# Expert gate and up matrices of two experts in one 4 MB load, and a TensorE loop over the two pairs of a turn

## The reference

```python
def run_block(args):
    xb, e = args
    h = jax.nn.silu(xb @ w_gate[e]) * (xb @ w_up[e])   # w_gate[e], w_up[e]: 1024 x 512
    return h @ w_down[e]                               # w_down[e]: 512 x 1024
y = jnp.zeros((N, D), x.dtype).at[slot_tok].add(ys * slot_gate[:, None])
```

## Time and profile before

| what | value |
|---|---|
| median of 3 runs | 1482.35 us (1481.81 to 1485.76) |
| the profiled execution | 1482.48 us |
| its span, first to last instruction | 1480.7 us |
| TensorE busy | 1235.6 us, 83% |
| VectorE, ScalarE busy | 496.0 us, 293.6 us |
| bytes read by DMA | 491.39 MB |
| mean granted TensorE clock | 0.946 of full |

### The profile page before, as it was taken

One profiled execution on the slowest core, in us unless ns is written; L12 is line 12 of the kernel. 1 busy time (PEld: TensorE's weight loads), 2 busy tenths in 40 slices (PEclk: granted clock), 3 DMA queues, 4 the chain that ended last, 5 costly groups with the idle time before them and its releaser, 6 DMA issues.

```text
span 1480.7 us, 34399 instructions
## 1 busy us (share of the span) xinstructions
PE 1235.6 (83%) x15164; PEld 947.1 (64%) x15164; DVE 496.0 (33%) x1038; ACT 293.6 (20%) x740; POOL 53.2 (4%) x89
## 2 busy tenths in 40 slices
PE   9999977677767777686777786877799999999998
PEld 6566756556556556565555565655678687888854
DVE  1663222122121120221221202212278555566644
ACT  3433221012021120210111202101232222211100
POOL 4101000000000000000000000000010110000000
PEclk9999999899899997998999989989999999999999
DMA  9539999999999999999999999999993351555420
GB/s 343 193 140 380 381 428 428 428 428 428 428 429 428 429 428 429 428 429 428 429 428 428 428 428 429 428 428 428 408 336 114 128 184 59 171 171 170 171 85 29
DMA packets 79759, 493.01 MB, mean 333 GB/s; under 512 B 4924, under 2 KB 28696, under 8 KB 55144
## 3 DMA queue, kind: packets, MB, share of 16 engines
q1 hardware_dynamic: 77792, 486.69, 80.1%
q0 software_dynamic: 1520, 4.91, 1.1%
q10 hardware_dynamic: 408, 0.86, 0.2%
HBM read 491.39 MB, written 1.05 MB: 333 GB/s over the span
## 4 chain that ended last, share of the span: by engine, by line
DMA 53%; PE 44%; DVE 1%; issue 1%; ACT 0%; POOL 0%; SPq 0%; DVEq 0%; POOLq 0%
DMA ring<-in_w_gate_dram 46%; PE bank L1678 8%; PE bank L1230 6%; DMA ring<-in_w_down_dram 5%; PE bank L881 4%; PE bank L1725 4%; PE bank L1358 4%; PE bank L1043 2%; DMA ring<-in_w_up_dram 2%; PE bank L1544 1%; PE bank L805 1%; PE bank L1654 1%; PE bank L1407 1%; PE bank L781 1%; PE bank L1587 1%; PE bank L1624 1%
## 5 line engine op out<-in xcount | busy, mean ns | idle before, releaser
L1230 PE MATMUL bank<-ring,big 128*32 128x128 f32 x8192 | 302.6, 309 | 176.0 <-DMA ring<-in_w_gate_dram 117.6
L1230 PEld LDWEIGHTS bank<-ring,big 128*32 128x32 f32 x8192 | 261.3, 125 | 226.8 <-DMA ring<-in_w_gate_dram 89.0
L2592 DVE TENSOR_TENSOR big<-big,bank 128x128 f32<-128x128 f32 x64 | 24.1, 376 | 498.5 <-PE bank L1230 498.5
L1259 PE MATMUL bank<-ring,big 128*32 128x256 f32 x1536 | 101.0, 406 | 33.6 <-DMA ring<-in_w_down_dram 33.1
L1982 ACT ACTIVATE big<-bank 32x256 f32<-32x256 f32 x96 | 35.9, 374 | 388.9 <-PE bank L1259 387.7
L2604 DVE COPY big<-bank 32x256 f32<-32x256 f32 x96 | 40.5, 422 | 195.7 <-PE bank L1259 194.2
L1259 PEld LDWEIGHTS bank<-ring,big 128*32 128x32 f32 x1536 | 50.3, 114 | 65.0 <-issue 28.3
L1245 PEld LDWEIGHTS bank<-aux,c 128*128 128x128 f32 x512 | 65.5, 200 | 15.0 <-issue 15.0
L1245 PE MATMUL bank<-aux,c 128*128 x512 | 74.3, 290 | 0.0
L881 PE MATMUL bank<-ring,xT 128*128 128x512 f32 (+1 forms) x160 | 67.9, 563 | 0.2 <-DVE xT L2231 0.2
L1205 PE MATMUL bank<-big,xn 128*128 128x128 f32 x512 | 65.1, 288 | 0.0
(11 more groups left out here) (482 smaller groups left out, 1691.3 us busy)
## 6 DMA issues: line engine op xcount, KB each, us to landing
ring<-in_w_up_dram SPq DMA_DIRECT2D x64, 2048.0 KB, 26.8
ring<-in_w_gate_dram SPq DMA_DIRECT2D x63, 2048.0 KB, 26.0
ring<-in_w_down_dram SPq DMA_DIRECT2D x62, 2048.0 KB, 27.1
ring<-in_w_gate_up_dram SPq DMA_DIRECT2D x22, 1024.0 KB, 7.7
ring<-in_w_down_dram SPq DMA_DIRECT2D x14, 1024.0 KB, 6.9
ring<-in_w_in_dram SPq DMA_DIRECT2D x12, 1024.0 KB, 14.8
ring<-in_w_in_dram SPq DMA_DIRECT2D x3, 2048.0 KB, 25.1
ring<-in_w_out_dram SPq DMA_DIRECT2D x2, 2048.0 KB, 18.5
```

What stands on the lines that cost most here:

```text
L1230: i = pe.matmul(dst[TOK * j:TOK * (j + 1), 0:P], xg[:, k, TOK * q:TOK * (q + 1)], w[:, k, j * P:(j + 1) * P], start=(k == 0), stop=(k == K ...
L1259: i = pe.matmul(bank[6 + q % 2][TOK * m:TOK * (m + 1), 0:SEQ], hT[:, q % 2, TOK * k:TOK * (k + 1)], w[:, k, SEQ * m:SEQ * (m + 1)], start= ...
```

## The change

- Order of the units: gate of both experts of a pair, up of both, down of each (`MOE_UNITS`). Gate and up of a pair come in one DMA of 4 MB into two adjoining slots (`two_slots`): partition p < 64 takes 16 successive rows of the first expert's matrix, p >= 64 of the second's, one run of 32 KB each (`pair_rows`). The first pair's still come as halves (runs of 16 KB), the second gate pair in pieces of 1, 1 and 2 MB. Down matrices come as before, the last one of a turn no longer in two halves.
- `hidden` multiplies a pair: 16 steps of k, four column tiles and two row tiles (64 rows x 32 columns each), the two experts in two banks.
- Gathers by pair: 16 k of 64 columns in two column tiles (128 x 64), one expert each, 32 slots wide, all in bank 2; the second pair of a turn is gathered in the turn's first half. `sel_now` holds the pair's selection. VectorE alone scales it into `xg`.
- TensorE runs a loop over the two pairs (h = 0, 1) with conditions for what one of them has only; memory rows all four ahead of the second gate product. Products with the identity stand where the array changes its form or a bank is taken again.
- The prologue gathers in the new form; `moe_gain` is loaded by two small DMAs on GpSimd's queue.

```diff
-MOE_UNITS = [(part, q) for q in range(BATCH) for part in ("gate", "up", "down")]
+MOE_UNITS = [(part, 2 * h + r) for h in range(BATCH // 2) for part in ("gate", "up", "down") for r in range(2)]
+            def pair_rows(part, experts):
+                return t_in["w_" + part][0, experts].rearrange("e (p k) c -> (e p) (k c)", p=HALF)
             def moe_load(u, expert):
+                if part == "down":
+                    sp.dma_start(slot(PRE_UNITS + u), ...)
+                else:
+                    sp.dma_start(two_slots(u), pair_rows(part, expert)).then_inc(S(f"moe_in{u % RING}"), 16)
...
-            def last_load(expert):
...
-            def first_gather(t, half):
+            def first_gather(t):
+                for k in range(KH):
+                    for r in range(2):
+                        i = pe.matmul(bank[2][HALF * r:HALF * r + HALF, k * TOK:(k + 1) * TOK],
+                                      xn[:, t, k * HALF:(k + 1) * HALF], sel[:, t, r * TOK:(r + 1) * TOK],
...
-                def hidden(part, q, dst, signal):
+                def hidden(part, h, dst, signal):
+                    arrive(part, h)
...
+                    w = two_slots(MOE_UNITS.index((part, 0))).rearrange("p (k c) -> p k c", k=KH)
+                    pe.matmul(dst[0][:, 0:P], ident, ident, start=True, stop=True)
+                    for k in range(KH):
+                        if part == "gate" and k in (4, 8):
+                            i.then_inc(S("moe_g0"), 1)
                         for j in range(4):
+                            for r in range(2):
+                                o = HALF * r
+                                i = pe.matmul(dst[r][TOK * j:TOK * (j + 1), 0:P], xg[o:o + HALF, k, :],
+                                              w[o:o + HALF, k, j * P:(j + 1) * P], start=(k == 0), stop=(k == KH - 1),
+                                              tile_position=(o, TOK * j))
...
+                def next_gather(h):
+                    pe.wait_ge(*at("moe_sel", it * 2 + h + 2))
+                    pe.wait_ge(*at("moe_xadd", it * 4 + 4))
+                    pe.matmul(bank[2][:, 0:P], ident, ident, start=True, stop=True)
+                    for k in range(KH):
+                        for t in range(TT):
+                            for r in range(2):
+                                i = pe.matmul(bank[2][HALF * r:HALF * r + HALF, k * TOK:(k + 1) * TOK],
+                                              xn[:, t, k * HALF:(k + 1) * HALF], sel_now[:, t, r * TOK:(r + 1) * TOK], ...)
...
-                for q in range(BATCH):
...
-                down_half(0)
-                down_half(1)
+                with pe.Fori(0, BATCH // 2) as h:
+                    with pe.If(h > 0):
+                        for q in range(4):
+                            memory_rows(q)
+                        pe.wait_ge(*at("moe_y_a", it * (2 * BATCH) + 4))
+                        pe.wait_ge(*at("moe_y_v", it * (2 * BATCH) + 4))
+                        pe.matmul(bank[7][:, 0:P], ident, ident, start=True, stop=True)
+                    hidden("gate", h, (bank[0], bank[1]), "moe_g")
+                    with pe.If(h < 1):
+                        ...                                  # transposes of sel_gate, as before
+                    hidden("up", h, (bank[5], bank[7]), "moe_gu")
+                    next_gather(h)
+                    down(h, 0)
+                    down(h, 1)
                 combine(0, 0)
```

More of the change, by code:

```diff
@@ L1188, in _ @@
             pe.wait_ge(*at("moe_sel", 0))
-            for half in range(2):
-                first_gather(0, half)
+            first_gather(0)
             pe.wait_ge(*at("picked", 2))
@@ L1196, in _ @@
             pe.wait_ge(*at("moe_sel", 1))
[L1197 to L1207, removed]
+            first_gather(1).then_inc(S("moe_xg_mm"), 1)
             pe.wait_ge(*at("rounds_ready", 1))
@@ L1212, in _, with arrive @@
                 it = c * NB + b
-                def arrive(part, q):
-                    u = MOE_UNITS.index((part, q))
-                    pe.wait_ge(*at(f"moe_in{u % RING}", it * 32 + 16 * (u // RING + 1)))
-                def hidden(part, q, dst, signal):
[L1220 to L1225, removed]
+                def arrive(part, h, r=0):
+                    u = MOE_UNITS.index((part, r))
+                    pe.wait_ge(*at(f"moe_in{u % RING}", it * 32 + h * 16 + 16))
@@ new lines, in next_gather @@
+                def next_gather(h):
[4 more added lines that the diff above has]
+                        for t in range(TT):
+                            for r in range(2):
+                                i = pe.matmul(bank[2][HALF * r:HALF * r + HALF, k * TOK:(k + 1) * TOK],
+                                              xn[:, t, k * HALF:(k + 1) * HALF], sel_now[:, t, r * TOK:(r + 1) * TOK],
+                                              start=(t == 0), stop=(t == TT - 1))
+                    i.then_inc(S("moe_xg_mm"), 1)
@@ L1982, in _ @@
                         A(y_batch[TOK * q:TOK * (q + 1), SEQ * m:SEQ * (m + 1)],
                           bank[6 + q % 2][TOK * m:TOK * (m + 1), 0:SEQ], ACT.Copy).then_inc(S("moe_y_a"), 1)
+                silu(0)
+                silu(1)
+                rows(0)
+                rows(1)
+                act.wait_ge(*at("cvw_in", 48))
+                act.wait_ge(*at("ckw_in", 96))
+                for home, kept in homes:
+                    A(kept, home, ACT.Copy)
+                silu(2)
@@ L1984, in _ @@
+                silu(3)
+                rows(2)
+                rows(3)
+                for home, kept in homes:
+                    i = A(home, kept, ACT.Copy)
+                i.then_inc(S("moe_v_ev"), 1)
             for t in range(TT):
```

249 lines of the change are left out of this document (96 added, 153 removed).

## The result

The kernel changed takes 1499.05 us (median of 4 runs, 1496.03 to 1500.62) against 1482.97 us of the kernel before, measured beside it: 1.0103 times as long, 95% interval 1.0080 to 1.0126. The forecast was 1481.8 us and a range up to 1489. The profiled execution took 1500.31 us with a span of 1498.5, so 17.8 us more span than before.

A forecast was written before the change was run, and what follows sets the result against it. The DMA stream of expert weights was taken to bound the kernel, with TensorE hidden in the turns. 1482.5 - 4.6 (rate) + 1.4 (start) + 2.6 (end) = 1481.9 us profiled, 1481.8 us as median; range 1477 to 1489.

The forecast's parts named there:

- The rate: Expert loads: 32 KB rows in place of 16 KB save 75 ns on each of 61 pair loads, 4.6 us less.
- Rival 2: Expert loads: 32 KB rows move no faster than 16 KB ones, giving 1486.5 us; chance 0.10.
- rival 3: Longer rows win more and TensorE stays at full clock at the end, giving 1477 us; chance 0.17.
- TensorE's turn: Expert turns: TensorE's work sums to 42.5 us, under 58.4, so the DMA stream hides it and it costs nothing.
- Rival 1: Expert products: eight tiles don't run together, records start 27 ns apart; 1496 us, or about 1599 with slow gather; chance 0.11.
- The start: Prologue's gather and first expert product: +1.0 us for the whole gather, +0.4 for later first pieces; +1.4 us (0.5 to 3).
- rival 4: TensorE's loop and conditions stall for instructions in the turns; from 3 us a branch about 1498 us; chance 0.04.
- As long as now: TensorE's loop: a body of 1576 records in place of 1556, so no new instruction packets were expected.
- 6.8 ns an instruction: Pair product: what eight tiles need (109/16); the sequencer was read as taking under 5 ns each, so fast enough.
- The slots: Expert turns: gate slots are freed at 3.5 to 6 us, at least 12 us of cover, so the stream stays fed.
- The end: Behind the last landing: +1.6 us for whole last down and copies, +1.0 for late TensorE; +2.6 us.
- The half clock: Last pair's up product: after idling TensorE runs at a granted clock of 0.50, so 1.5 us were added to up.

The follow-up runs named there:

- the unrolled loop: Changed kernel with the loop over the two pairs written out in place of `pe.Fori`: 1855.90 us, 1.2512.
- 132 instructions of shift: Kernel before with 33 identity products ahead of the expert loop: 1514.34 us (1.0208) with products of 7.5 us in all, 1520.94 us (1.0253) with products of 128x16.
- The delays put into the kernel before: Kernel before with products of 128x64 ahead of the expert loop: 64 of them (256 instructions) 1496.78 us, 1.0093; 16 of them (64 instructions) 1486.30 us, 1.0021.
- The kernel with wide tiles: Changed kernel with the old 128x32 tiles, gather form and 16 KB rows, keeping new order, pair loop and slots freed by pairs: 1490.13 us, 1.0051.
- the kernel moved by 64: Changed kernel with 16 products of 128x64 (64 instructions) ahead of its loop: 1494.20 and 1502.05 us in two executions, then 1495.94 us, 1.0086, in five more.
- the execution of 1502.05 us: One of the first two executions of the changed kernel with 64 instructions ahead of its loop; the other took 1494.20 us.

## Why the prediction was wrong

**The rate** was right: 431 GB/s for the 432 forecast, from a line through two row sizes. Rival 2 is refuted by the rate; rival 3 too, and by the end, where up ran below full clock.

**TensorE's turn** was right: 3.78 us for the pair product (3.5 and an end of 0.3), 3.92 for the gather (3.7), all under the turn of 58.4. Rival 1 fell. The mean start of 14.8 ns also settles the place where the Trainium skill (TensorE: Matmul & The Clock Gate, Back-to-back issue gap) spoke against the change: its floor of about 25 ns doesn't hold between tiles.

**The start** is the step that failed: +1.4 forecast, 18.8 us of shortfall measured. Of its own terms the gather was sound (64 records took 1.99 us where I had 1.9); the others can't be told apart in the first turn as it ran. What it left out is that this is the one turn whose code is new. I had looked for instruction packets from 300 to 700 us, where a loop that stays in the engine shows none, and priced rival 4 as a cost of branches in each turn. "As long as now" counted records; what matters in the first turn is how long a packet lasts, and 6.8 ns an instruction was a number of the prediction itself. It stood there as proof that the sequencer keeps up, from a stretch whose code was in the engine already. The kernel before has the telling rows too, a wait of 0.52 us inside a product at 164.62 and instruction packets every 6 to 9 us: a fetch that was all but hidden. Rival 4 named 1498 us, with stalls of 3 us for branches in every turn; from 240 to 1060 us only 0.6 us of TensorE's waits are put down to issue. That its number is near the measured one is luck.
The Trainium skill (Runtime: NRT & Kernel Launch, Instruction fetch mechanics) has the crossing of a 16 KB block mostly hidden, because engines dispatch more slowly than blocks come, and it warns of taken branches and says that kernels prefer full unrolling. The runs disagree in both: straight code was broken in mid-product, up to 3.2 us at a time, the branches of the later turns cost 0.6 us in all, and the unrolled loop took 1855.9 us. It also gives TensorE room for 2048 instructions. That bodies of some 1,570 stayed and one of 3,100 didn't agrees with it; that 132 instructions of shift made a difference isn't explained by it.

**The slots** follow from it: 12 us of cover was worked out for steady turns and held there. In the first turn the ring is full and nothing is queued behind it, so each microsecond of TensorE stops the stream. The delays put into the kernel before pass on one for one (13.9 us late gave 13.3 us, 3.1 gave 3.1).

**The end** was mis-sized: +4.3 for +2.6. The half clock was foreseen, at 1.5 us; up took 5.74 for 3.78, so 2.0, and 1.2 more are identity products (L1238, L1255) that the step forgot. The kernel with wide tiles shows this part with hardly any shortfall, 3.0 us.

## What to carry to other kernels

Count instructions where code runs for the first time, and how long the engine takes over 256 of them. At 1.9 us, less than the 2.3 us of a fetch, the waits summed to 11.8 us here and much of what followed ran at half clock; at 3.9 us they summed to 0.6 in the kernel before, and to 0.8 to 2.3 where its code was moved. A fetch can show there too, so this is a warning and not a rule. An edit of engine code also moves all code behind it; before a difference of 1 or 2% is put down to the edit, look for instruction packets inside the loop. A bound that holds in steady turns says nothing of the first, where the ring has no lead; a price for the start needs rows of the start.

## What the runs showed of the hardware

- A packet of instructions holds 256; where TensorE waited for one in the changed kernel, it went on 2.2 to 2.4 us after the packet started.
- A loop of some 1,560 instructions stayed in TensorE or was fetched anew in each turn (8.5 packets, some 1.8 us a turn) by where it began: in the kernel before, moved by 64 or 256 it stayed, by 132 it didn't. Of one twice as long 229 packets were fetched.
- Ahead of the loop 33 products of 128x16 lasted 10.2 us (155 ns a record), 33 of 128x128 7.5 us and 16 of 128x64 3.7 to 3.8 us (118): a narrower product was no shorter. The granted clock was 0.72 around the narrowest (148 to 160 us) and 1.00 around the 64 products of 128x64 (111 ns a record), which accounts for the difference.
- The changed kernel's times spread over 4.6 us in 4 runs, with its code moved by 64 over 1.0 in 5 (though over 7.9 in the two of the other group), the kernel before over 1.8 in 13 of one group and 4.0 in the 4 of the first.
- The first turn's waits are not the same in each execution. The wait in L1197 was 1.05 us in one trace of the kernel moved by 64 and 1.42 in the other (8.1 and 8.0 us of waits in all), and 1.30 to 2.42 us in seven kernels whose code is the same up to there. No trace of the execution of 1502.05 us was kept.
